# Twelve 256-column chunks with a two-part accumulator for six 512-column chunks, in a two-block transformer layer

## The reference

```python
proj = x @ w_in_mix                       # 256 x 1024 times 1024 x (1024 z, 1536 xbc, 16 dt, 1024 B, 1024 C, 1024 h)
xbc = silu(causal_depthwise_conv(xbc, ssd_conv_w) + ssd_conv_b)      # 4 taps, over tokens, each column by itself
y   = state_space(xbc, dt, ...) * silu(z), normalised, times ssd_norm_w
s   = B * causal_depthwise_conv(C * h, sc_conv_w)                    # 3 taps
mix = concatenate([y, s]) @ w_out_mix
x   = layer_norm(ALPHA * x + mix)         # then feed-forward, a gated embedding, and an attention layer of the same kind
```

## Time and profile before

| | us |
|---|---|
| median of 3 runs (1212.45 to 1212.87) | 1212.52 |
| the profiled execution | 1212.66 |
| its span, first to last instruction | 1210.6 |
| TensorE busy | 1204.3 |
| GpSimd busy | 852.8 |
| ScalarE busy | 679.3 |
| VectorE busy | 668.7 |

### The profile page before, as it was taken

How to read it: one execution, slowest core, us unless ns; L and a number is a source line. 1 busy time by engine, 2 the same in 40 slices (tenths; PEclk the granted TensorE clock), 3 DMA queues, 4 the chain that set the end, 5 groups by cost and what they waited for, 6 DMA issues and landing times.

```text
span 1210.6 us, 18515 instructions
## 1 busy us (share of the span) xinstructions
PE 1204.3 (99%) x7367; PEld 1044.1 (86%) x7367; DVE 668.7 (55%) x1152; ACT 679.3 (56%) x913; POOL 852.8 (70%) x369
## 2 busy tenths in 40 slices
PE   9999999999999999999999999999999999999998
PEld 8987888888888888899999888888889878888887
DVE  6847546331256689646662255536753674544865
ACT  6873757655476755546544464445556666444543
POOL 7977468649978800968589788883777548998174
PEclk9999999999999999999999999999999999999999
DMA  9756355537756646746466766664648446676462
GB/s 303 215 159 172 109 154 157 156 89 222 212 152 196 191 165 217 213 130 189 127 176 215 256 195 188 182 197 164 228 144 280 139 120 169 187 205 190 158 225 70
DMA packets 147772, 218.32 MB, mean 180 GB/s; under 512 B 9392, under 2 KB 79591, under 8 KB 147687
## 3 DMA queue, kind: packets, MB, share of 16 engines
q1 hardware_dynamic: 144295, 209.92, 57.1%
q10 hardware_dynamic: 3392, 7.23, 1.8%
HBM read 216.08 MB, written 1.05 MB: 179 GB/s over the span
## 4 chain that ended last, share of the span: by engine, by line
PE 99%; ACT 0%; DMA 0%; DVE 0%; issue 0%; DVEq 0%; ACTq 0%
PE acc L2285 18%; PE acc L2292 9%; PE acc L2322 9%; PE acc L2324 9%; PE acc L2323 9%; PE pm L2338 5%; PE acc L2329 4%; PE acc L2331 4%; PE acc L2332 4%; PE acc L2757 3%; PE acc L2756 3%; PE acc L2758 3%; PE acc L2251 2%; PE acc L2253 2%; PE acc L2252 2%; PE acc L2500 1%
## 5 line engine op out<-in xcount | busy, mean ns | idle before, releaser
L642 POOL TENSOR_TENSOR wlo<-raw,whi 128x1024 fp32r<-128x1024 f32 (+4 forms) x362 | 847.5, 2371 | 345.3 <-ACT whi L656 230.6
L656 ACT ACTIVATE whi<-raw 128x1024 fp32r<-128x1024 f32 (+4 forms) x404 | 403.6, 1022 | 209.1 <-PE acc L2292 52.2
L2285 PE MATMUL acc<-XT,whi 128*128 128x512 f32 x960 | 229.9, 391 | 0.4 <-DVE XT L1226 0.4
L2285 PEld LDWEIGHTS acc<-XT,whi 128*128 128x128 f32 x960 | 176.2, 188 | 35.3 <-issue 0.8
L2292 PEld LDWEIGHTS acc<-XT,wlo 128*128 128x128 f32 x960 | 123.3, 191 | 4.9
L2292 PE MATMUL acc<-XT,wlo 128*128 128x256 f32 x960 | 124.8, 283 | 0.0
L2322 PE MATMUL acc<-whi,XT 128*128 128x512 f32 (+4 forms) x296 | 112.6, 380 | 0.1
L2329 PE MATMUL acc<-XT,whi 128*128 128x256 f32 x392 | 111.9, 285 | 0.0
L2331 PE MATMUL acc<-XT,whi 128*128 128x256 f32 x392 | 110.9, 283 | 0.0
L2332 PE MATMUL acc<-XT,wlo 128*128 128x256 f32 x392 | 110.9, 283 | 0.0
L2324 PE MATMUL acc<-whi,XT 128*128 128x512 f32 (+4 forms) x296 | 110.1, 372 | 0.0
(11 more groups left out here) (537 smaller groups left out, 2278.1 us busy)
## 6 DMA issues: line engine op xcount, KB each, us to landing
raw<-in_w_in SPq DMA_DIRECT2D x68, 512.0 KB, 3.8
raw<-in_w_ff SPq DMA_DIRECT2D x64, 512.0 KB, 3.8
raw<-in_w_gate SPq DMA_DIRECT2D x44, 512.0 KB, 4.0
raw<-in_w_up SPq DMA_DIRECT2D x44, 512.0 KB, 3.9
raw<-in_w_down SPq DMA_DIRECT2D x44, 512.0 KB, 3.8
raw<-in_w_in_mix SPq DMA_DIRECT2D x36, 512.0 KB, 3.6
raw<-in_w_branch SPq DMA_DIRECT2D x16, 512.0 KB, 3.8
raw<-in_w_out_mix SPq DMA_DIRECT2D x16, 512.0 KB, 3.3
```

Source lines behind the costliest of these rows:

```text
L642: nc.gpsimd.tensor_tensor(piece(wlo, u), piece(raw, u), piece(whi, u).bitcast(F32), ALU.subtract).then_inc(S["w_lo"], 1)
L656: return nc.scalar.activation(out_, in_, func, **k)
L2285: T.matmul(acc[:, n % 2, f, :], piece(whi, u)[:, i, f * P:(f + 1) * P], XT[:, :, k, :], start=k == 0, stop=False)
```

## The change

xbc0 and xbc1 become four B chunks (xbc00, xbc01, xbc10, xbc11), and sb0, sc1, sh1 and sb1 become eight (sb00 to sb11). xbc2, sc0 and sh0 stay F. Each new chunk's two parts are added on VectorE: a copy of the second part to `part_sums` (the buffer `em`), then a sum in place, or for sc1 straight into `scc`, which ScalarE filled before. The convolutions and the products run on two tiles at a time, and the high and low halves of the short outputs are made by quarters. Order and place in each engine's list stay as they are, apart from the splitting.

```diff
--- before.py
+++ after.py
@@ -96,6 +96,10 @@
     def gates(i):
         for c in range(2):
             g.append((f"gate{i}_{c}", "w_in", KD, O_GATE + i * D + c * W, W, "T"))
+
+    def halves(name, at):
+        for h in range(2):
+            g.append((f"{name}{h}", "w_in_mix", KD, at + h * HW, HW, "B"))
 
     def branch(i):
         for c in range(2):
@@ -118,12 +122,18 @@
     for c in range(3):
         if c == 2:
             g.append(("dt", "w_in_mix", KD, M_DT, SSD_H + ZA, "T"))
-        g.append((f"xbc{c}", "w_in_mix", KD, M_XBC + c * W, W, "F"))
+        if c < 2:
+            halves(f"xbc{c}", M_XBC + c * W)
+        else:
+            g.append(("xbc2", "w_in_mix", KD, M_XBC + c * W, W, "F"))
     for c in range(2):
         g.append((f"mz{c}", "w_in_mix", KD, ZA + c * ZB, ZB, "T"))
     for c in range(2):
         for n, o in (("sc", M_C), ("sh", M_H), ("sb", M_B)):
-            g.append((f"{n}{c}", "w_in_mix", KD, o + c * W, W, "F"))
+            if (n, c) in (("sc", 0), ("sh", 0)):
+                g.append((f"{n}{c}", "w_in_mix", KD, o + c * W, W, "F"))
+            else:
+                halves(f"{n}{c}", o + c * W)
     for part, k0 in (("a", KD), ("b", 0)):
         for c in range(2):
             g.append((f"mo{c}{part}", "w_out_mix", KD, c * W, W, "T", k0))
@@ -542,6 +552,7 @@
             n, _, _, _, w, _, _ = chunks[name]
             return acc[:, n % 2, 0:w // P, part * TOK:(part + 1) * TOK]
 
+        part_sums = em[:].rearrange("p h r s -> p h (r s)").rearrange("p h (f t) -> p h f t", t=TOK)
         f1s = pm[:, 3, :].rearrange("p (f t) -> p f t", t=TOK)
         hm = pm[:, 3, :].rearrange("p (f t) -> p f t", t=TOK)
         def last_gate(j):
@@ -985,14 +996,14 @@
             act.dma_start(pin[:], a["p0"].rearrange("(t p) d -> p t d", p=P)).then_inc(S["p_in"], 16)
             high_halves(landed("f2_1") + AHEAD)
             turn("x3", XThi, first=2)
-            high_halves(landed("xbc1") + AHEAD)
+            high_halves(landed("xbc11") + AHEAD)
 
             def silu2(j):
-                act.wait_ge(*evac_at(f"xbc{j}"))
+                act.wait_ge(*evac_at(("xbc01", "xbc11", "xbc2")[j]))
                 fn(xbcT[:, 4 * j:4 * j + 4, :], xbcT[:, 4 * j:4 * j + 4, :], ACT.Silu).then_inc(S["silu2"], 1)
             silu2(0)
             turn("p0", PThi)
-            high_halves(landed("xbc1") + AHEAD)
+            high_halves(landed("xbc11") + AHEAD)
             silu2(1)
             high_halves(landed("dt") + AHEAD)
             logs()
@@ -1036,12 +1047,10 @@
             squares(2)
             link(squares(3))
             rstd(rs[:, 0:4], ss[:, 0:4], W, eps5).then_inc(S["y_ss"], 1)
-            for c in range(2):
-                if c:
-                    leave("sc1", scc[:])
-                high_halves(landed(f"sb{c}") + AHEAD)
-                act.wait_ge(S["c_out"], c + 1)
-                fn(BYhi[:, 8 + 4 * c:12 + 4 * c, :], accF(f"sb{c}"), ACT.Copy).then_inc(S["c_hi"], 1)
+            for n in range(4):
+                high_halves(landed(f"sb{n // 2}{n % 2}") + AHEAD)
+                act.wait_ge(S["c_out"], n + 1)
+                fn(BYhi[:, 8 + 2 * n:10 + 2 * n, :], accB(f"sb{n // 2}{n % 2}", 0), ACT.Copy).then_inc(S["c_hi"], 1)
             high_halves(landed("mo1a") - 1 + AHEAD)
             turn("y", BYhi[:, 0:8, :], lambda f: bcol("ssd_norm_w", f))
 
@@ -1795,11 +1804,18 @@
             def by_head(ap):
 
                 return ap.rearrange("p (h d) -> p h d", d=SSD_D)
-            for j in range(3):
-                v.wait_ge(S["w_used"], landed(f"xbc{j}"))
+            def parts_added(name, h, out_=None):
+
+                v.wait_ge(S["w_used"], landed(name))
+                link(V.tensor_copy(part_sums[:, h], accB(name, 1)))
+                return V.tensor_tensor(accB(name, 0) if out_ is None else out_, accB(name, 0), part_sums[:, h], ALU.add)
+
+            def convolved(name, view, first):
+
+                n = view.shape[1]
                 for back in range(4):
-                    for f in range(4 * j, 4 * j + 4):
-                        w, x = bcol("ssd_conv_w", 12 * (3 - back) + f), accF(f"xbc{j}")[:, f % 4, 0:TOK - back]
+                    for f in range(first, first + n):
+                        w, x = bcol("ssd_conv_w", 12 * (3 - back) + f), view[:, f - first, 0:TOK - back]
                         if back == 0:
                             last = V.tensor_scalar(xbcT[:, f, :], x, w, bcol("ssd_conv_b", f), ALU.mult, ALU.add)
                         else:
@@ -1807,7 +1823,15 @@
                                                           in1=xbcT[:, f, back:], op0=ALU.mult, op1=ALU.add)
                     if back < 3:
                         link(last)
-                last.then_inc(evac_at(f"xbc{j}")[0], 1)
+                last.then_inc(evac_at(name)[0], 1)
+            for j in range(3):
+                if j < 2:
+                    for h in range(2):
+                        link(parts_added(f"xbc{j}{h}", h))
+                        convolved(f"xbc{j}{h}", accB(f"xbc{j}{h}", 0), 4 * j + 2 * h)
+                else:
+                    v.wait_ge(S["w_used"], landed("xbc2"))
+                    convolved("xbc2", accF("xbc2"), 8)
                 if j == 1:
                     turn("p0", PThi, PTlo)
                     v.wait_ge(S["w_used"], landed("dt"))
@@ -1852,16 +1876,13 @@
             link(V.tensor_tensor(by_head(off), by_head(off), per_head(eac[:, 0, :]), ALU.mult))
             V.tensor_tensor(yd[:, 1, :], off, yd[:, 1, :], ALU.add).then_inc(S["s_yod"], 1)
 
-            def short_input(c):
-
-                v.wait_ge(S["w_used"], landed(f"sh{c}"))
-                v.wait_ge(*evac_at(f"sc{c}"))
-                gated = accF(f"sh{c}")
-                link(V.tensor_tensor(gated, gated, scc[:], ALU.mult))
+            def short_input(name, c, gated, tiles):
+
+                link(V.tensor_tensor(gated, gated, scc[:, tiles], ALU.mult))
                 for back in range(3):
-                    for f in range(4):
+                    for f in range(tiles.start, tiles.stop):
                         w = bcol("sc_conv_w", 8 * (2 - back) + 4 * c + f)
-                        x = gated[:, f, 0:TOK - back]
+                        x = gated[:, f - tiles.start, 0:TOK - back]
                         if back == 0:
                             last = V.tensor_scalar(scv[:, f, :], x, w, None, ALU.mult)
                         else:
@@ -1869,18 +1890,22 @@
                                                           op0=ALU.mult, op1=ALU.add)
                     if back < 2:
                         link(last)
-                last.then_inc(evac_at(f"sh{c}")[0], 1)
+                last.then_inc(evac_at(name)[0], 1)
 
             def short_output(c):
-                v.wait_ge(S["w_used"], landed(f"sb{c}"))
-                v.wait_ge(*evac_at(f"sh{c}"))
-                V.tensor_tensor(accF(f"sb{c}"), accF(f"sb{c}"), scv[:], ALU.mult).then_inc(S["c_out"], 1)
-                v.wait_ge(S["c_hi"], c + 1)
-                V.tensor_tensor(BYlo[:, 8 + 4 * c:12 + 4 * c, :], accF(f"sb{c}"),
-                                BYhi[:, 8 + 4 * c:12 + 4 * c, :].bitcast(F32), ALU.subtract)\
-                    .then_inc(evac_at(f"sb{c}")[0], 1)
-                v.wait_ge(*evac_at(f"sb{c}"))
-                V.engine_nop().then_inc(S["c_lo"], 1)
+
+                for h in range(2):
+                    n, name = 2 * c + h, f"sb{c}{h}"
+                    link(parts_added(name, h))
+                    v.wait_ge(*evac_at(("sh0", "sh1" + str(h))[c]))
+                    V.tensor_tensor(accB(name, 0), accB(name, 0), scv[:, 2 * h:2 * h + 2], ALU.mult)\
+                        .then_inc(S["c_out"], 1)
+                    v.wait_ge(S["c_hi"], n + 1)
+                    V.tensor_tensor(BYlo[:, 8 + 2 * n:10 + 2 * n, :], accB(name, 0),
+                                    BYhi[:, 8 + 2 * n:10 + 2 * n, :].bitcast(F32), ALU.subtract)\
+                        .then_inc(evac_at(name)[0], 1)
+                    v.wait_ge(*evac_at(name))
+                    V.engine_nop().then_inc(S["c_lo"], 1)
 
             def decays(hb):
                 c, first = hb // 4, 8 * (hb // 2 % 2) + 4 * (hb % 2)
@@ -1920,7 +1945,9 @@
                 if hb < 6:
                     decays(hb + 2)
             finished(3)
-            short_input(0)
+            v.wait_ge(S["w_used"], landed("sh0"))
+            v.wait_ge(*evac_at("sc0"))
+            short_input("sh0", 0, accF("sh0"), slice(0, 4))
             v.wait_ge(S["y_ss"], 1)
             link(half_variance(0, 4, ss[:, 0:4], W, 1e-5))
             refine_columns(0, 4)
@@ -1929,7 +1956,12 @@
                 last = V.tensor_scalar(y4[:, k, :], y4[:, k, :], rs[:, k:k + 1], None, ALU.mult)
             last.then_inc(S["y_n"], 1)
             short_output(0)
-            short_input(1)
+            for h in range(2):
+                parts_added(f"sc1{h}", h, scc[:, 2 * h:2 * h + 2]).then_inc(evac_at(f"sc1{h}")[0], 1)
```

(20 more changed lines are left out.)

## The result

The changed kernel takes 1218.84 us (median of 6 runs, 1217.97 to 1219.59) against 1212.51 (6 runs, 1212.22 to 1212.87): 1.0052 times, 95% interval 1.0041 to 1.0062. It is 6.3 us slower. The profiled execution took 1219.59 us with a span of 1217.8 us from its first to its last instruction; before, 1212.66 and 1210.6.

The account below looks back on a forecast made before the run. TensorE, busy 1204.3 of 1210.6 us, was taken as the bound. Terms -2.3 + 1.2 + 0 + 1.0 + 3.8 + 0.1 for weight-load restarts gave +3.8 us, 1216.3 us, range 1213.7 to 1219.2.

Parts of the forecast that it names:

- Pace: Twelve B chunks at 5.57 us instead of 5.76 us per 256 output columns: saves 2.3 us.
- Wait 1: At the head of xbc00, TensorE waits for the transposed x3: 1.2 us, bounds 1.0 to 1.4.
- Evacuation of xbc00 to xbc11: VectorE empties each chunk at 5.35 us against 5.57 available: cost 0, bounds 0 to 0.6 us.
- Wait 2: At sb01, TensorE waits for the accumulator of sh0: 1.0 us.
- Wait 3: At sc10, TensorE waits for sb00's accumulator, behind VectorE's refinement and scaling of y: 3.8 us, the main term.
- Rival D: GpSimd's subtractions hold all four scalings of y, so sc10 waits 8.1 us: 1220.6 us; chance 0.05.
- rival C: The 3.8 us of idle before sc10 costs TensorE's clock, 2.4 us: 1218.7 us; chance 0.14.
- Rival A: GpSimd's six subtractions end by 613.6, so the wait before sc10 is 1.3 us: 1213.8 us; chance 0.11.
- Rival B: Evacuations stay hidden because a VectorE step is not waited for: 1210.2 to 1211.5 us; chance 0.05.

Follow-up runs that it names:

- e3_interleave: The changed kernel with the first unit of xbc01 moved before the second unit of xbc00: 1221.79 us.
- e6_ahead: The changed kernel with ScalarE allowed two more weight units before the first short output, so GpSimd has eight subtractions in a row, not six: 1223.92 us.
- e5_warm8: The changed kernel with 8 extra 512-column matmuls into an unused PSUM bank right before sc10: 1216.85 us.
- e1_warm: The changed kernel with 15 extra 512-column matmuls into an unused PSUM bank right before sc10: 1217.42 us.
- e9_short: The kernel before with only sb0, sc1, sh1 and sb1 split, xbc0 and xbc1 left as before: 1218.60 us.
- e3_turn: The changed kernel with the last transposes of x3 between the high and low pass of xbc00's first unit, ScalarE's copies ahead of its next weight copy: 1216.99 us.
- e7_sb0F: The changed kernel with x3's transposes moved between xbc00's passes, VectorE's list reordered, and sb0 left one F chunk with refinement ahead of its output: 1211.67 us.

## Why the prediction was right, and where it fell short

- Pace: right. 5.57 us a chunk in both stages, -2.3 us.
- Wait 1 (1.2 forecast, 1.0 to 1.4): 1.30. Evacuation of xbc00 to xbc11 (0): right, no wait. VectorE took from 516.15 to 521.34 for xbc00 in the changed kernel, 5.19 against the 5.15 of the sum, and e3_interleave shows the same length as a wait of 2.5 where 2.55 was worked out.
- Wait 2 (1.0): 0.99.
- Wait 3 (3.8 from the due time): 3.63. The step that carried it, six subtractions instead of eight and so three free scalings, is shown by e6_ahead in the other direction. (The sum took 2.38 us for a subtraction where its own row gives 2.42; here the six took 14.19 us, 2.37 each.) Rival D's price (8.1) is what e6_ahead measured as 7.7.
- The sum without the clock, 1216.3, is near what the kernel does if its clock is held: the medians of e5_warm8 and e1_warm are 1216.85 and 1217.42, 0.5 and 1.1 above it.
- The point forecast was 2.5 us low. What the sum lacks is the term of rival C, the clock. It was put at nothing in the sum and given 0.14; its price was 2.4 us and its time 1218.7, and measured are 2.65 us in the profiled execution and 1218.84. The mechanism had been named, the weight was wrong, and the time fell inside the range only because rival C's price had been added to its upper end. That 2.4 was so close is luck in part: it was taken between the bounds 1.5 and 3.2, and the five traces with such a fall show 1.6 to 2.8.
- How often it falls: in four of the six runs of the changed kernel the mean clock is 0.997 or 0.998, which no run of the kernel before has. The other two have 0.999, which proves nothing by itself: e9_short's profile has 0.999 with a fall, and some runs of the kernel before have it too. The trace of before had no idle stretch of TensorE over 1.3 us, so it could not say what one of 3.8 us would do.
- The Trainium skill's rule ("TensorE: Matmul & The Clock Gate", What's actually happening), that an idle engine goes to half its clock, is what happened here, with 0.50 in the window behind the wait. In e3_turn the fall came 0.7 us after TensorE had begun to work again (last section), and 1.6 and 2.5 us of idle time brought none. The forecast had left this rule, which spoke against the change, to a rival.
- Rival A fell: GpSimd was busy until 618.57. Rival B fell: each of the three semaphores was waited for.

## What to carry to other kernels

A chunk that is half as long gives its accumulator half the time to be emptied. For each new chunk list what stands ahead of its evacuation (taking its result out of PSUM) in the evacuating engine's own order, also what has nothing to do with it: here 13 instructions of another branch, nine of the refinement and four scalings, which had delayed nothing before, decided the result, and moving them gave 5.6 of the 6.3 us back. When a sum ends in an idle stretch of TensorE like the 3.5 us here, add the slow clock behind it as a term (1.6 to 2.8 us in these traces), not as a rival.

## What the runs showed of the hardware

The price of the clock varies with the execution. Behind the same wait of 3.5 us sc10 took 8.22 us (changed kernel), 8.33 (e3_interleave), 7.28 (e3_turn) and 7.17 (e9_short), and behind 7.7 us it took 7.84 (e6_ahead), against 5.57 at full clock. Idle stretches of 1.1 (changed kernel), 1.6 (e5_warm8) and 2.5 us (e3_interleave) cost none in the profiled executions. The price is about half of the time that TensorE works at the lower clock, and the fall does not always come while it idles. In the changed kernel it came 1.3 us before sc10 began. In e3_turn sc10 began at 622.79 and the clock fell only after that (TensorE's windows):

```profile
622.00:623.00 1.00, 0.21 (x1) 1.00 0.00 0
623.00:624.00 1.00, 1.00 (x4) 0.76 0.00 0
```

TensorE worked at the lower clock from about 623.5 to 626.9 there, which cost 1.7 us, and in the changed kernel for 5.5 us, which cost 2.65. The longer wait of e6_ahead did not cost more clock: 2.3 us.

The first 10 us vary too. TensorE in e1_warm (profiled 1216.73 us):

```profile
5.87 2.11 PE L2390 MATMUL pm<-ct,X 128*128 128x128 f32 x14
7.81 1.02 PE L2383 MATMUL acc<-dn 128*128 128x512 bf16 x4
```

and in e5_warm8 (profiled 1218.19 us):

```profile
6.02 3.25 PE L2390 MATMUL pm<-ct,X 128*128 128x128 f32 x14
9.06 1.76 PE L2383 MATMUL acc<-dn 128*128 128x512 bf16 x4
```

The same instructions run at half the pace for longer, which shifts everything behind by 1.7 us, though the granted clock reads 1.00 for this stretch in both. The kernel before does the same for a shorter time. So in these first microseconds the pace is that of the lower clock while the record shows the higher one. Of the twelve profiles ten have the group that follows the second line above at 8.65 to 8.90 us, e9_short has it at 10.23 and e5_warm8 at 10.42. The same distance separates 5 of 58 executions of the kernel before (1214.14 to 1214.49) from the rest (1212.22 to 1213.05), and the two groups of e7_sb0F; that the start is the cause there too is likely but not shown, as those executions have no trace. Single executions of such a kernel can thus differ by almost 2 us before the change is reached.
